# Low parts of the w_up_2 units made by minus-high parts and adding DMAs, in two halves that TensorE awaits apart

## What is computed

```
h2 = rmsnorm(x, mlp_norm_w[l])
u = jax.nn.relu(jnp.einsum('bld,df->blf', h2, w_up[l]))      # 1024 -> 4096
x = x + jnp.einsum('blf,fd->bld', u * u, w_down[l])           # 4096 -> 1024
return rmsnorm(x, final_norm_w)
```

## Time and profile before

| | us |
|---|---|
| median of 3 runs (1566.85 to 1567.38) | 1567.03 |
| the profiled execution, as timed | 1569.01 |
| its span, first to last instruction | 1566.9 |
| TensorE busy in the span | 1550.7 |
| granted TensorE clock, share of full speed | 0.998 |

### The profile page before, as it was taken

The page is one execution under the profiler, slowest core; times in us unless marked ns, Lnnn a source line. Parts: engine busy times, 40 slices in busy tenths (PEclk is TensorE's granted clock), DMA queues, the critical chain, the costliest instruction groups (busy, mean ns, idle before and its releaser), DMA issues.

```text
span 1566.9 us, 19248 instructions
## 1 busy us (share of the span) xinstructions
PE 1550.7 (99%) x7495; PEld 1279.0 (82%) x7495; DVE 914.3 (58%) x1185; ACT 533.1 (34%) x760; POOL 725.1 (46%) x289
## 2 busy tenths in 40 slices
PE   9999999999999999999999999999999999999997
PEld 6887788888888988888888897887778988888886
DVE  5901589820074566666301578997764436585878
ACT  3012211210124434344213435227643343333444
POOL 5875189687762254444544001441124263645551
PEclk9999999999999999999999999999999999999999
DMA  6242023233234223333224032331124164536462
GB/s 229 81 134 81 1 88 107 68 121 108 81 108 134 81 81 108 92 95 107 84 105 142 29 108 60 103 96 40 28 82 153 37 187 137 146 91 184 88 188 81
DMA packets 132885, 159.57 MB, mean 102 GB/s; under 512 B 5527, under 2 KB 98759, under 8 KB 132808
## 3 DMA queue, kind: packets, MB, share of 16 engines
q1 hardware_dynamic: 125430, 141.05, 28.4%
q0 software_dynamic: 5504, 12.58, 4.5%
q10 hardware_dynamic: 1874, 4.85, 0.9%
HBM read 152.18 MB, written 2.10 MB: 98 GB/s over the span
## 4 chain that ended last, share of the span: by engine, by line
PE 86%; POOL 6%; issue 4%; DVE 2%; ACT 2%; DMA 1%; POOLq 0%; DVEq 0%; SPq 0%; ACTq 0%
PE ps L849 26%; PE ps L850 26%; PE ps L851 26%; PE ps L1004 3%; PE ps L1079 2%; POOL w_lo L834 1%; PE ps L1246 1%; POOL w_lo L773 1%; PE ps L1067 1%; POOL w_lo L832 1%; PE ps L1263 1%; POOL tail_lo L834 1%; POOL w_hi L768 1%; PE ps L1138 1%; POOL tail_lo L832 0%
## 5 line engine op out<-in xcount | busy, mean ns | idle before, releaser
L773 POOL TENSOR_TENSOR w_lo<-raw,w_hi 128x1024 fp32r<-128x1024 f32 x166 | 420.5, 2554 | 497.8 <-ACT w_hi L1349 495.0
L849 PE MATMUL ps<-hT_hi,w_hi 128*128 128x512 f32 (+1 forms) x848 | 325.2, 383 | 1.1 <-POOL w_lo L773 0.5
L850 PE MATMUL ps<-hT_lo,w_hi 128*128 128x512 f32 (+1 forms) x848 | 323.7, 382 | 0.0
L851 PE MATMUL ps<-hT_hi,w_lo 128*128 128x512 f32 (+1 forms) x848 | 323.6, 382 | 0.0
L768 POOL TENSOR_TENSOR w_hi<-raw,cells 128x2048 fp32r<-128x2048 f32 x35 | 129.6, 3703 | 126.3 <-PE ps L849 125.2
L849 PEld LDWEIGHTS ps<-hT_hi,w_hi 128*128 128x128 f32 x848 | 159.7, 188 | 34.6 <-issue 2.3
L851 PEld LDWEIGHTS ps<-hT_hi,w_lo 128*128 128x128 f32 x848 | 159.7, 188 | 30.9
L850 PEld LDWEIGHTS ps<-hT_lo,w_hi 128*128 128x128 f32 x848 | 159.8, 188 | 30.1
L1349 ACT ACTIVATE w_hi<-raw 128x2048 fp32r<-128x2048 f32 (+1 forms) x58 | 109.7, 1891 | 128.6 <-PE ps L849 106.5
L849 PE MATMUL ps<-w_hi,hT_hi 128*128 128x512 f32 (+2 forms) x400 | 151.6, 379 | 0.5 <-POOL w_lo L792 0.5
L850 PE MATMUL ps<-w_lo,hT_hi 128*128 128x512 f32 (+2 forms) x400 | 150.1, 375 | 0.0
(11 more groups left out here) (368 smaller groups left out, 3054.3 us busy)
## 6 DMA issues: line engine op xcount, KB each, us to landing
raw<-in_w_in SPq DMA_DIRECT2D x86, 512.0 KB, 4.6
raw<-in_w_up SPq DMA_DIRECT2D x54, 512.0 KB, 4.7
raw<-in_w_down SPq DMA_DIRECT2D x38, 512.0 KB, 4.5
raw_tail<-in_w_up SPq DMA_DIRECT2D x22, 512.0 KB, 4.7
raw<-in_w_out SPq DMA_DIRECT2D x16, 512.0 KB, 4.2
raw_tail<-in_w_down SPq DMA_DIRECT2D x16, 512.0 KB, 5.8
raw<-in_w_ret_o SPq DMA_DIRECT2D x8, 512.0 KB, 4.0
raw<-in_w_sgu_o SPq DMA_DIRECT2D x8, 512.0 KB, 4.1
```

What stands on the lines that cost most here:

```text
L773: nc.gpsimd.tensor_tensor(lo[:, c], raw[:, s, c], hi[:, c].bitcast(f32), ALU.subtract).then_inc(unit_split, 1)
L849: first = nc.tensor.matmul(dst, a_hi, b_hi, start=start, stop=False, skip_group_check=onto)
L850: nc.tensor.matmul(dst, a_hi, b_lo, start=False, stop=False, skip_group_check=onto)
L851: return first, nc.tensor.matmul(dst, a_lo, b_hi, start=False, stop=stop, skip_group_check=onto)
```

## The change

The low part of the 14 up units of `STREAM` is no longer a subtraction by POOL. ACT writes `-hi` into the low buffer, in two halves, right after hi, and POOL's queue issues two DMAs that add the raw buffer onto it, `lo = -hi + raw`, one for each half as it is ready. Each slot and half has a semaphore of its own, and TensorE awaits the first half ahead of the first matmul of the unit and the second half ahead of its 13th, in which the first of the second four blocks is used. SP, which reloads the raw buffer, awaits both halves. Down products are made as before.

```diff
 def low_count(v):
-    by_vector = [kind == "down" and n in VECTOR_LOW for kind, _, n in STREAM]
-    return by_vector[v], by_vector[:v + 1].count(by_vector[v])
+    maker = [2 if kind == "up" else 1 if n in VECTOR_LOW else 0 for kind, _, n in STREAM]
+    if maker[v] == 2:
+        return 2, len([w for w in range(v % W_SLOTS, v + 1, W_SLOTS) if maker[w] == 2])
+    return maker[v], maker[:v + 1].count(maker[v])
...
+        def await_low_half(engine, v, half):
+            engine.wait_ge(tail_low_dma[v % W_SLOTS][half], 16 * low_count(v)[1])
...
             # POOL, for each unit v of STREAM
+                if maker == 2:
+                    n_up = [w for w in range(v + 1) if STREAM[w][0] == "up"].index(v)
+                    for half in range(2):
+                        c = slice(half * UNIT // 2, (half + 1) * UNIT // 2)
+                        pool.wait_ge(tail_negated, 2 * n_up + half + 1)
+                        pool.dma_start(lo[:, c], tail_raw_of(v)[:, c],
+                                       accum_op=ALU.add).then_inc(tail_low_dma[v % W_SLOTS][half], 16)
+                    continue
...
             # TensorE, up2_unit
-                await_low(pe, v)
...
                     for kk in range(KT):
+                        if c == 0 and kk % 4 == 0:
+                            await_low_half(pe, v, kk // 4)
...
             # ACT, tail_high
                 nc.scalar.activation(tail_slot(v)[0], tail_raw_of(v), ACT.Copy).then_inc(tail_hi, 1)
+                if kind == "up":
+                    act.wait_ge(tail_hi, v + 1)
+                    for half in range(2):
+                        c = slice(half * UNIT // 2, (half + 1) * UNIT // 2)
+                        nc.scalar.activation(tail_slot(v)[1][:, c], tail_slot(v)[0][:, c].bitcast(f32), ACT.Copy,
+                                             scale=-1.0).then_inc(tail_negated, 1)
```

More of the change, by code:

```diff
@@ L560, in two_blocks @@
         tail_low = [sem("tail_low_pool"), sem("tail_low_dve")]
+        tail_low_dma = [[sem(f"tail_low_dma{s}_{half}") for half in range(2)] for s in range(W_SLOTS)]
+        tail_negated = sem("tail_negated")
         tail_started = sem("tail_started")
@@ L595, in raw_part @@
             return tail_raw[PLACE["down", q, HELD[name]]]
+        def await_low_half(engine, v, half):
+            engine.wait_ge(tail_low_dma[v % W_SLOTS][half], 16 * low_count(v)[1])
         def await_low(engine, v):
-            by_vector, n = low_count(v)
-            engine.wait_ge(tail_low[by_vector], n)
+            maker, n = low_count(v)
+            if maker == 2:
+                for half in range(2):
+                    await_low_half(engine, v, half)
+            else:
+                engine.wait_ge(tail_low[maker], n)
         block = ctx.enter_context(nc.Block())
@@ L827, in _ @@
                     sum_by_dma(q, "T4", raw_part(q, "T2").rearrange("p (k n) -> p k n", k=4))
-                if low_count(v)[0]:
+                maker = low_count(v)[0]
+                if maker == 1:
                     continue
                 hi, lo = tail_slot(v)
+                if maker == 2:
+                    n_up = [w for w in range(v + 1) if STREAM[w][0] == "up"].index(v)
[5 more added lines that the diff above has]
+                    continue
                 pool.wait_ge(tail_hi, v + 1)
@@ L2334, in _ @@
                     token_low(at_v + 2)
-                    if low_count(at_v + 2)[0]:
+                    if low_count(at_v + 2)[0] == 1:
                         weight_low(at_v + 2)
```

## The result

The changed kernel takes 1575.29 us in the median of 5 runs (1574.38 to 1577.93), the kernel before 1567.19 (5 runs, 1566.85 to 1567.38). The ratio is 1.0053, with an interval of 1.0042 to 1.0064: slower, by 8.1 us between the medians and 8.3 by the ratio. The forecast was 1571.1 with a range of 1565.5 to 1576.0, so the sign holds, the median lies in the range, and the size falls 4.2 us short. The profiled execution is timed 1574.43.

A forecast was written before the change was run, and what follows sets the result against it. TensorE was taken to bound the last stage, nearly without gaps. Terms 1.45 + 2.25 + 1.6 - 1.2 = 4.1 us on the span of 1566.9 gave 1571.0, plus 0.1 for the median: 1571.1, range 1565.5 to 1576.0.

The forecast's parts named there:

- Behind T3: At up(2,1) and up(3,1): first adding halves queue behind T3's DMAs on POOL's queue, costing 1.45 and 2.25 us.
- Beside SP's loads: At up(1,3), up(2,3), up(3,3): adds share the DMA engines with SP's load bursts, 0 to 4.8 us, taken as 1.6.
- the upper bound: At up(2,3): equal shares delay the first half 2.6 us, less 1.2 in hand, and the second some 0.6: 2.0 in all.
- equal shares everywhere: Rival: adds share equally with the loads at all three up(q,3) units, 4.8 us there, total 1574.3 us; chance 0.18.
- priced at nothing: ACT's 28 extra halves, POOL's 28 fewer pieces, later raw buffers and reloads, and T4 about 2 us later: 0 us.
- What is won: At up(2,2) and up(3,2): DVE's token sum shortens without POOL's pieces, rounding comes sooner, lateness and slow restarts go: 1.2 us.
- a longer handover: Rival: at all nine tight up units the handover exceeds 8.2 us by more than 1.2; about 1580 us; chance 0.10.
- the price named for the load of an up(q,3) unit: T4 of quarter 0 lands about 2 us later, so up(1,3)'s load just meets its rounding and would be next late.
- the base of the sum: Profiled span 1566.9 us before the change; the median of runs, 1567.03, stands 0.1 above it, so 0.1 was added.

The follow-up runs named there:

- both edits: Changed kernel with T3 issued at down(q,2) instead of down(q,1) and SP's down(q,0) loads held until up(q,3)'s low part, q = 1 to 3: 1569.84 us.

## Why the prediction came out as it did

**Behind T3: right in kind, 1.1 too high.** Forecast 1.45 + 2.25; measured, with restarts, 1.38 + 1.17 = 2.55, and nil with T3 moved. It is 2.57 of the stage where nothing else is in play (both edits against the loads held alone). The step itself, a queued half after T3's last, measured 2.46 and 2.71 us against the 2.6 taken from the earlier trace rows. What was off is where TensorE stood at up(3,1): it wanted the unit 4.0 us later in the stage than before (4.6 of new waits and restarts, less 0.6 won), while T3 landed only 2.8 later, so T3 landed 1.8 us before the wanted matmul, not 0.5. Lateness at one unit is slack for the next.

**Beside SP's loads: the term that was mis-sized.** Forecast 1.6 out of bounds of 0 and 4.8; measured, with restarts, 0.99 + 2.25 + 2.42 = 5.7 in the profiled execution; the lateness alone is 5.3 there, and 6.8 and 7.4 in the two others, half clock not counted. Two choices in that step failed. First, "two of the three meet only the tail of the loads": all three were hit. At up(1,3) the first add took 6.9 us from issue to landing, at up(2,3) 8.1 and at up(3,3) 7.5, where it takes 4.7 undisturbed. Secondly, the upper bound was "equal shares, so that the first half takes 2.6 us more": at up(2,3) it took 3.4 more, and in the other traces of this kernel up to 3.9. At a DMA share of 1.05 to 1.07 the row of free engines is no bound on what a DMA beside the burst takes. The rival "equal shares everywhere" (1574.3, chance 0.18) is thus what came nearest, not the likeliest case. That its number meets the profiled execution's 1574.43 is partly luck: it has 1.1 too much behind T3 and 0.9 too little beside the loads, and that the engines share equally isn't shown. Where the loads are held the cost is 0. Of the 5.7, some 0.8 isn't the sharing but the late rounding of up(3,3), which stood under "priced at nothing" (below); by itself it fits in the time in hand, as the unit starts on time with the loads held.

**What is won: right.** Forecast 1.2, measured 1.24, and 1.28 in the stage with no add in the kernel at all. The chain is the one described, by its rows (DVE, then ACT at up(2,2)):

```profile
1366.22 4.42 DVE L2326 SCALAR_TENSOR_TENSOR f<-f 128x1024 f32<-128x1024 f32 x1
```

```profile
1390.02 1.90 ACT L1722 ACTIVATE tail_hi<-raw_tail 128x2048 fp32r<-128x2048 f32 x1
```

4.42 where I wrote about 5; the rounding stands 9.4 us ahead of its unit, where it had 7.3. With POOL back on up(2,1) it is 9.13: whenever POOL subtracts beside the sum, the sum takes twice as long. The Trainium skill (SBUF — State Buffer, Who interferes with whom) says that VectorE and GpSimd shut each other out where VectorE reads two inputs and GpSimd reads too. These numbers agree with it.

**Priced at nothing: right where engines are free.** The handover at up(1,1): ACT's start at 1284.29, the adds issued at 1287.6, the first landed 4.7 later.

```profile
1284.29 1.90 ACT L1722 ACTIVATE w_hi<-raw_tail 128x2048 fp32r<-128x2048 f32 x1
1286.22 2.01 ACT L1727 ACTIVATE w_lo<-w_hi 128x1024 fp32r<-128x1024 f32 x2
```

```profile
L848 POOL DMA_DIRECT2D w_lo<-raw_tail x2: 861/881/901, 1287.6 to 1288.5; - x2
...
DMA to landing us min/median/max: 4.7/5.4/6.2
```

That is 8.0 us against 8.2 forecast, so the rival of a longer handover falls. ACT's 28 halves and the later reloads cost no unit of quarters 1 and 2; the price named for the load of an up(q,3) unit came up at up(3,3). T4 of quarter 2 lands at 1492.2, SP issues the load behind it, and the rounding waits for that:

```profile
1492.24 0.92 SPq L747 DMA_DIRECT2D raw_tail<-in_w_up  x2
```

```profile
1497.60 1.92 ACT L1722 ACTIVATE w_hi<-raw_tail 128x2048 fp32r<-128x2048 f32 x1 [0.71 <-DMA raw_tail<-in_w_up]
```

The second half is there 2.5 us after the first (6.2, issued 0.9 later, against 4.7), as T4's rows said. By the price of the Trainium skill (DMA: Bandwidth & Descriptors, Anatomy of one DMA) it would be 1.2, an estimate from its bytes. The measurement again says twice that.

**Not foreseen: TensorE's clock.** No term of the sum had it. The profiled execution shows none and the sum of its terms is 7.0 us; the two other traces lose 1.7 and 3.4 us to it. With the five runs between 1574.4 and 1577.9, the median above the profiled time fits what the traces show, longer waits beside the loads and half clock behind some. The granted clocks go the same way, 0.999 in the three fastest runs and 0.998 and 0.997 in the two slowest; but for the runs without a trace it is argued, not shown. The run that is the median (1575.29) is one of those at 0.999, so longer waits alone are the likelier cause there.

**That the range held is in part luck.** Two of the five runs (1577.1 and 1577.93) and both further executions (1577.55 and 1579.67) lie above its end of 1576.0. And the base of the sum was right by chance: times stand some 2 us above spans (1574.43 and 1572.4), so the median before, 1567.03, is not a run with a span of 1566.9. Most of the 2 us was made up by the half clock of the profiled execution at 1065.7 us (3.4 us of it, so 1.7 lost).

So of the 4.2 us between forecast and median, 4.1 stand at the three units beside the loads (0.8 of it by the late rounding of up(3,3)), -1.1 is T3, and some 1.2 are left for the executions that wait longer than the profiled one.

## What to carry to other kernels

A DMA that stands on the critical path has the price of its row only while nothing else is in flight. Before moving engine work to one, lay its issue times beside the windows of DMA share: here five of the nine tight uses had a burst or another DMA of the same queue beside them, and lost 7.7 us where the four others lost none. Where a new wait falls on TensorE, add a term for the half clock that can follow it (1.7 us for each 3.4 us stretch here).

The thing won, DVE freed of POOL's company, was to be had without a DMA: two low parts moved to DVE give 1565.60, 1.4 us under the kernel before and 9.7 under the changed one.

## What the runs showed of the hardware

- Adding DMAs of 128x1024, on-chip buffer onto on-chip buffer: 4.6 to 4.7 us from issue to landing alone; the next one queued lands 2.5 to 2.7 after it. Beside a burst of loads, at a DMA share of 1.05 to 1.08, the first takes 6.9 to 8.1 in the profiled execution and up to 8.8 in the other traces; at up(1,3) it took 6.9, 7.1, 7.3 and 8.6 in four traces of the same program up to there.
- VectorE's token sum of 128x1024: 4.42 and 4.45 us without GpSimd's subtractions beside it, 9.13 and 9.15 with them.
- TensorE at the half level of its clock (1.2 of 2.4 GHz) for 3.4 us after standing still, at granted clocks of 0.50 to 0.56 in the windows shown: behind waits of 2.35, 2.58, 2.88, 3.18, 3.24, 3.31, 3.52, 3.73, 4.13, 4.35 and 4.39 us; once (T3 later, 3.03) for 6.8 us. Not behind 2.13, 2.34, another 2.35 and 2.60, nor behind a 3.11 and a 3.70. So the length of the wait alone doesn't decide it, and what else does stays open.
